# One decoder layer with 32 experts on one Trainium2 core: the first round of the expert stage in another order

## The reference, cut to what matters

```python
g_logits = (x @ w_rg + b_rg);  _, g_idx = lax.top_k(g_logits, 1)
e_logits = (x @ w_re + b_re).reshape(N, 4, 8)
e_sel = take_along_axis(e_logits, g_idx[:, :, None], axis=1)[:, 0]
e_val, e_idx = lax.top_k(e_sel, 2)
e_w = softmax(e_val) * take_along_axis(softmax(g_logits), g_idx)
for e in range(32):
    h = jax.nn.silu(x @ w_eg[e]) * (x @ w_eu[e])
    out = out + combine[:, e:e + 1] * (h @ w_ed[e])
```

## Time and profile before

| | us |
|---|---|
| median of 3 runs | 718.13 (714.38 to 722.01) |
| profiled execution, its own time | 714.71 |
| its span, first to last instruction | 712.9 |
| first matmul of the expert rounds, in the span | 143.40 |
| first slot of the ring loaded anew, in the span | 149.48 |
| last weights of experts issued | 629.06 |

### The profile page before, as it was taken

The page is one execution under the profiler, slowest core; times in us unless marked ns, Lnnn a source line. Parts: engine busy times, 40 slices in busy tenths (PEclk is TensorE's granted clock), DMA queues, the critical chain, the costliest instruction groups (busy, mean ns, idle before and its releaser), DMA issues.

```text
span 712.9 us, 8954 instructions
## 1 busy us (share of the span) xinstructions
PE 659.5 (93%) x2874; PEld 454.9 (64%) x2874; DVE 549.0 (77%) x595; ACT 478.3 (67%) x439; POOL 92.9 (13%) x123
## 2 busy tenths in 40 slices
PE   9999998789999999989999999898989899998895
PEld 4566554367767686766767677675767576674342
DVE  2265125948999999999999999998989899994543
ACT  3200203649878888798887979897877888881253
POOL 4000001200021120202202021120202020210000
PEclk9999999989999999999999999999999999999998
DMA  9993304359999999999999999999999999874401
GB/s 304 391 300 118 119 29 156 139 228 407 419 409 427 421 414 425 404 416 409 416 412 419 416 409 404 414 399 404 410 373 408 412 390 397 349 280 174 145 15 59
DMA packets 30750, 232.36 MB, mean 326 GB/s; under 512 B 8694, under 2 KB 10046, under 8 KB 17925
## 3 DMA queue, kind: packets, MB, share of 16 engines
q1 hardware_dynamic: 25277, 226.09, 79.4%
q0 software_dynamic: 4480, 5.26, 2.2%
q10 hardware_dynamic: 976, 0.79, 0.3%
HBM read 231.76 MB, written 10.37 MB: 340 GB/s over the span
## 4 chain that ended last, share of the span: by engine, by line
PE 50%; DMA 25%; DVE 10%; issue 9%; ACT 4%; DVEq 0%; POOLq 0%; SPq 0%; ACTq 0%; POOL 0%
DMA moe_rows<-yo,cur 18%; PE ps L841 9%; PE ps L842 8%; DMA ring<-in_w_eg_dram 6%; PE ps L915 5%; PE ps L752 5%; PE ps L856 5%; DVE lo L1429 5%; PE ps L844 4%; ACT hi L1024 3%; PE ps L653 2%; PE ps L660 2%; PE ps L647 2%; DVE yo L1422 2%; PE ps L614 2%
## 5 line engine op out<-in xcount | busy, mean ns | idle before, releaser
L1024 ACT ACTIVATE hi<-ring 128x2048 fp32r<-128x2048 f32 x192 | 318.4, 1698 | 24.1 <-PE ps L842 6.7
L1429 DVE TENSOR_TENSOR lo<-ring,hi 128x2048 fp32r<-128x2048 f32 (+1 forms) x128 | 256.2, 2022 | 27.4 <-ACT hi L1024 13.2
L841 PE MATMUL ps<-hi,xr 128*128 128x512 f32 x448 | 194.8, 435 | 17.1 <-DVE lo L1429 14.4
L1429 DVE TENSOR_TENSOR lo_third<-ring,hi 128x1536 fp32r<-128x1536 f32 (+1 forms) x64 | 129.3, 2020 | 6.5 <-ACT hi L1024 5.9
L842 PE MATMUL ps<-lo,xr 128*128 128x512 f32 x320 | 127.1, 397 | 0.0
L841 PEld LDWEIGHTS ps<-hi,xr 128*128 128x128 f32 x448 | 85.4, 191 | 47.6 <-DVE lo L1429 21.1
L841 PE MATMUL ps<-hi,hr 128*128 128x512 f32 x224 | 91.0, 406 | 12.3 <-DVE lo L1429 9.6
L1033 ACT ACTIVATE gu<-ps 128x512 f32<-128x512 f32 x64 | 70.0, 1094 | 23.3 <-PE ps L844 23.3
L856 PEld LDWEIGHTS ps<-fold,gu 128*128 128x128 f32 x512 | 61.9, 192 | 21.8 <-issue 13.7
L559 POOL DMA_INDIRECT moe_rows<-yo,cur x16 | 35.2, 2199 | 300.3 <-DVE yo L1422 300.3
L842 PEld LDWEIGHTS ps<-lo,xr 128*128 128x128 f32 x320 | 61.4, 192 | 12.0
(11 more groups left out here) (234 smaller groups left out, 625.5 us busy)
## 6 DMA issues: line engine op xcount, KB each, us to landing
ring<-in_w_eu_dram SPq DMA_DIRECT2D x32, 2048.0 KB, 18.2
ring<-in_w_eg_dram SPq DMA_DIRECT2D x32, 2048.0 KB, 17.6
ring<-in_w_ed_dram SPq DMA_DIRECT2D x31, 2048.0 KB, 18.8
ring<-in_w_in_dram SPq DMA_DIRECT2D x2, 2048.0 KB, 17.2
ring<-in_w_out_dram SPq DMA_DIRECT2D x2, 2048.0 KB, 21.4
ring<-in_w_ple_gate_dram SPq DMA_DIRECT2D x2, 2048.0 KB, 10.2
ring<-in_w_in_dram SPq DMA_DIRECT2D x2, 1024.0 KB, 8.8
ring<-in_w_ed_dram SPq DMA_DIRECT2D x2, 1024.0 KB, 7.9
```

Source lines behind the costliest of these rows:

```text
L841: mm(out, parts, hi(u)[:, cut], start=begin, stop=False)
L1024: acti(hi(u), ring[:, u // 2, off:off + split(u)], ACT.Copy).then_inc(hi_ready, counted(u, first, last))
L1429: V.tensor_tensor(lo(u), ring[:, u // 2, off:off + split(u)], hi(u).bitcast(F32), ALU.subtract).then_inc(lo_ready, counted(u, first, last))
```

## The change

All edits are at the seam between routing and the rounds.

1. DVE writes the first pair's row numbers straight into `cur` (not `row_in`), and POOL issues the first gather without its own copy. The wait of `all_slots` on POOL's copy goes.
2. POOL zeroes the pads after it has issued the first gather, not before.
3. PE does `ple_product(2)` ahead of the places, `(3)` and `(4)` after the first pick, then turns the gathered rows, and only then does the 48 products for the other pairs and `ple_product(5)`.
4. ACT copies product 4 and then `xr` ahead of unit 3's high part and product 5. It waits for `rows_r` before the first copy of a gate product.
5. DVE does `low_x(0)` after unit 0's low part, ahead of unit 1's and of `all_slots`.
6. In the first step ACT copies the up product (`copy_gu` of unit 3) ahead of unit 7's high part.

```diff
-                pool.wait_ge(hn_out, 16 * TILES)
-                pool.wait_ge(cur_in, x + 1)
+                pool.wait_ge(cur_in, q * PAIRS + i)
                 pool.sem_inc(turns, 1)
+                gather_rows()
+
+            def gather_rows():
+
                 nc.gpsimd.indirect_dma_start(
                     xg[0:ODD_END, :], None, hn_rows,
...
                 slot_numbers()
+                pool.wait_ge(hn_out, 16 * TILES)
+                need(pool, x_done, q * ROUNDS)
+                pool.wait_ge(rows_r, 2 * q + 1)
+                pool.sem_inc(turns, 1)
+                gather_rows()
                 if isinstance(q, int):
-                    pool.wait_ge(hn_out, 16 * TILES)
                     zero(xr[:, :, :, :, SLOTS:HALF].bitcast(F32), xz[:, :, SLOTS:P],
                          h32[:, :, SLOTS:P], hr[:, :, :, SLOTS:HALF].bitcast(F32))
-                pool.wait_ge(rows_r, 2 * q + 1)
-                pool.sem_inc(turns, 1)
-                gather(q * ROUNDS, 0)
...
-            ple_product(0)
-            ple_product(1)
+            for n in range(3):
+                ple_product(n)
...
                 pick_slots(q, 0)
                 if isinstance(q, int):
-                    ple_product(2)
                     ple_product(3)
+                    ple_product(4)
+                    pe.wait_ge(most_r, 1)
+                turn_x(q * ROUNDS)
                 pick_slots(q, 1)
                 if isinstance(q, int):
-                    ple_product(4)
                     ple_product(5)
-                pe.wait_ge(most_r, 1)
-                turn_x(q * ROUNDS)
                 pe.wait_ge(pads, 1)
...
-                    for u in range(2):
-                        high(u)
-                        copy_ple(2 * u)
-                        copy_ple(2 * u + 1)
-                    high(2, 3)
+                    high(0)
+                    copy_ple(0)
+                    copy_ple(1)
+                    high(1)
+                    copy_ple(2)
+                    copy_ple(3)
+                    high(2)
                     copy_ple(4)
-                    copy_ple(5)
                     act.wait_ge(pads, 1)
                     high_x(n)
+                    high(3)
+                    copy_ple(5)
+                    act.wait_ge(rows_r, 2)
...
-                    high(6, 7)
+                    high(6)
+                    if not first:
+                        high(7)
                     copy_gu(n, x, 3)
+                    if first:
+                        high(7)
...
-                V.tensor_tensor(row_in[:, 0:1], r_a[:, 0:1], ps[:, FIRST_IDX, 1:2], ALU.add).then_inc(rows_r, 1)
+                V.tensor_tensor(cur[:, 0:1], r_a[:, 0:1], ps[:, FIRST_IDX, 1:2], ALU.add).then_inc(rows_r, 1)
...
-                dve.wait_ge(cur_in, q * ROUNDS + 1)
...
                     choose(1, PAIRS)
-                    low(0, 1)
+                    low(0)
+                    low_x(0)
+                    low(1)
                     all_slots(0, link)
                     dve.wait_ge(ple_s, 2 * TILES)
                     low(2)
-                    low_x(0)
```

More of the change, by code:

```diff
@@ L536, in slot_numbers, with gather @@
                 nc.gpsimd.memset(slot_no[:, SLOTS:HALF], -NOWHERE).then_inc(iota_s, 1)
-            def gather(x, i):
+            def gather(x, i, q):
                 need(pool, x_done, x)
@@ L567, in step @@
                 if not last:
-                    gather(n + 1, i + 1)
+                    gather(n + 1, i + 1, q)
                 if not first:
```

## The result

| | before | changed |
|---|---|---|
| median of 20 runs | 719.32 us (713.42 to 723.42) | 716.24 us (714.0 to 718.89) |
| ratio | | 0.9958, 95% interval 0.9941 to 0.9976 |
| profiled execution, own time (span) | 714.71 (712.9) | 716.06 (714.3) |

The change is 3.0 us faster (1.7 to 4.2), where I had forecast 5.2: a gain clear of noise, of 0.4% and not 0.7%. Timed again beside other kernels it gave 0.9934 (0.9904 to 0.9963). The profiled execution of the changed kernel is an ordinary one; that of before is one of its kernel's fastest (714.71 against a median of 719.32), and so it is the shorter of the two. Two things have to be taken apart in the trace.

A forecast was written before the change was run, and what follows sets the result against it. DMA engines, unbroken from SP's first refill (149.48 us), bound the kernel. Unit 0 3.65 us sooner plus 1.55 by the clock gives 5.2 off the 718.13 us median: 712.9 us, range 706 to 720.5.

The forecast's parts named there:

- The mechanism: Rounds: DMA engines work without a pause from the first refill, so the end comes sooner by as much, 5.2 us.
- Rival A: Rounds: compute engines are the bound to the end, so 6.7 us gained, 711.4 us, up to 8; chance 0.17.
- Rival B: First gather: DVE's compare holds off POOL, rows come at 137.6, only 3.3 us gained, 714.8 us; chance 0.13.
- the signs that I had named: Trace after: for example, forecast wrong if first refill moves by 5 us and last weights' issue (629.06) does not.
- Rival C: Rounds: longer queue lowers DMA rate from 416 to 403 GB/s, 7.1 us lost against 5.2 gained, 720.0; chance 0.10.
- PE: Routing: product 2, 1.8 us, fits ahead of the places; turn at 135.7, picks until 137.9, product 5 until 139.7.
- The gather 0.99 after the row numbers: First gather: without POOL's copy its DMA begins 0.99 us after DVE's write, at 131.2, so 0.8 us earlier.
- Turn, picks and product 5: PE before unit 0: turn 135.7 to 136.65, picks until 137.9, product 5 (1.79 us) until 139.7.
- Units 0 and 1: First units on PE: 4.32 us instead of 5.89 with no hole ahead, 1.55 us gained by the clock.
- Pads: POOL's 18 memsets behind the first gather, 1.7 us in all: cost 0 to 0.3 us, at worst 2.
- The second gather's copy: POOL's copy beside unit 2's low part may be held until 143.9; nothing lost, as PE wants the rows about 160.
- about 1%: Measurement: 7.2 us is what can be told from no change; chances 0.26 faster, 0.67 within 1%, 0.07 slower.

The follow-up runs named there:

- e5: Changed kernel with the first refill held back until unit 3 is done, engines' work unchanged; 718.76 us, 0.9993 of before.
- the light transfers: Refills of rounds 1 to 15 cut to three quarters of their bytes (results wrong): changed kernel 693.07 us, kernel before 704.31 us.
- e1: Changed kernel with product 2 behind the first pick again; 713.3 us, 0.9924 of before.
- e2: Kernel before with only POOL's part: row numbers straight to `cur`, first gather ahead of the pads, turn still last; 718.26 us, 0.9991 of before.
- e7b: Kernel before with slot 2's down matrix for round 1 loaded already at 77 us; 719.75 us, 1.0004 of before.
- e6: `e1` with unit 7's high part again ahead of the copy of unit 3's up product; 715.46 us, 0.9939 of before.
- e7: `e1` with slot 2's down matrix for round 1 loaded already at 77 us; 710.15 us, 0.9880 of before.
- p3: The changed kernel itself, three products ahead of the places, timed again in another job; 715.03 us, 0.9934 of before.
- w1: Changed kernel with two extra unit-matrix products on PE around turning the last tile of h, ahead of the routing; 715.69 us, 0.9936 of before.
- p4: Changed kernel with product 3 also ahead of the places, four in all; 719.79 us, 0.9986 of before.

## Why the prediction was wrong, and where it was right

**The mechanism held in the main.** The time goes with the first refill as long as no pause follows, and the engines' further lead turns into queue: landing times at 200 us rose from 13.2 to 18.0, and `e5` and the light transfers show it. Rival A (engines to the end, 6.7 or more) is refuted by them, and by ACT's waits, which grew (6.4 us to 8.9 for the up matrices). Rival B, GpSimd held off by VectorE's comparison, did not occur: the gather's instruction took 1.15 us, and rows moved at 74 to 205 GB/s from 136.5 us on, with the comparison running until 138.3. Of the signs that I had named, one came out against me: the first refill moved, and the last weights' issue did not (629.08 against 629.06). In the other traces it did (625.22 in `e1`, 633.18 in `e2`).

Rival C came in small. From 180 to 400 us the rate is 416 GB/s in both kernels, but split up, the changed kernel has 421 from 180 to 320 us and 408 from 320 to 440, where before has 417 and 413. Over 180 to 620 us that makes 409 against 410, so the changed kernel lost next to nothing by it. The lower rate goes with the queue: from 320 to 440 us it was 412 or 413 in the traces whose up matrices landed in 16 to 17 us at 300 to 330 us (before, `e2`, `e7b`, `e6`, `e7`), and 403 to 410 where that took 19 to 21. My argument that 13 and 22 us differ only in how many transfers wait left this out.

**The step that failed** is the first one under **PE**: product 2 ahead of the places, "so it fits", costed at nothing beyond its 1.8 us at the full clock. By length it did fit: three products at the full clock put the places 5.26 us after the first product (`p3`, `w1`), and I had counted on 5.59. But in the trace after, the clock stood at 0.50 from 125 to 128 us, the products took 7.11 us, and the places came at 6.95, 1.36 late. I had written of the clock for the units and not for this place. Row numbers and gather were late by as much, the turn by 1.1, since the gather took 4.1 us and not 4.5, unit 0 by 1.0 and the first refill by 0.9:

| us after the first product | forecast | trace after |
|---|---|---|
| places | 5.59 | 6.95 |
| gather begins | 8.85 | 10.18 |
| turn | 13.35 | 14.44 |
| unit 0 | 17.40 | 18.37 |
| first refill | 21.95 | 22.89 |

There was also something to be had that I did not see: with two products ahead the places stand at 4.9, because the cast of VectorE that took 0.84 us beside the memsets now took 0.17. The room is 1.2 us ([1.21 <-DVE] with two products ahead), not 1.9, for a product of 1.8. With product 2 back the gain is 5.5 us (3.4 to 7.6) in one job and 7.7 (5.7 to 9.7) in the other, around and above my 5.2.

The Trainium skill (SBUF — State Buffer, section Who interferes with whom) says that a cast of VectorE can run in a mode in which it and GpSimd's instructions exclude each other. The trace agrees: 0.84 us beside the memsets, 0.17 without. I had looked at that section for what it would cost behind the gather, and not for what it gave back ahead of it.

**Other terms.** The gather 0.99 after the row numbers: as assumed. Turn, picks and product 5: 0.96, 1.18 and 1.86 against 0.92, 1.19 and 1.79. PE stood still for 1.95 us before the turn, not "up to a microsecond". Units 0 and 1: from 142.88 to the end of the last matmul at 147.21, 4.33 against 4.32, at the full clock, in this trace; in `w1` and `p4` part of them ran at the halved clock. Pads: free. The second gather's copy took 1.98 us and ended at 146.86, with VectorE's subtraction at 146.81: foreseen, and free. My "about 1%" for what can be told from no change was too coarse: 20 runs of each tell 0.42% to within 0.18%.

**What stays open.** Whether the full DMA engines hold the kernel up through the weights, as I argued, or also through the scatter, on which ScalarE waits longer, is not parted by any run. Of the 2.2 us between forecast and medians, the trace places 0.9 at the first refill. The rest is within the interval (1.7 to 4.2 us), and no run here shows where it went: behind the first refill the traces differ by more than that, 479.6 against 481.7 us to the last issue, and 83.8 against 85.2 from there to the end, which the change doesn't touch. The clock's level changes from one execution to the next at places that no kernel here controls, so one trace each can't settle the last microsecond.

## What to carry to other kernels

When a long stretch is full of transfers, cost a change first by the instant at which the stretch begins and by the pauses inside it. To test that the transfers set the end, hold one back that no engine needs yet: moving the engines and the transfers together can't tell. A transfer moved ahead of the stretch helps only as far as its room doesn't turn into a pause. Room for extra work in an engine's gap is the gap after the change: ask what ended it, and whether the same change makes that earlier. Work put into a gap ahead of a short dependent step should be costed at both levels of the clock: products 0 and 1 took 3.70 us in some traces and 5.40 in others, in the same place of the list.

## What the hardware showed that I had not expected

Runs of one kernel differ through the granted clock. The 35 runs of before in the first job had mean granted clocks of 0.971 to 0.985, and a line fitted to their spans falls by 0.56 us for each 0.001 of clock (correlation -0.88). The lower level came at different places in different executions: from 60 to 70 us the mean was 0.67 in the changed kernel's trace and 1.00 in that of before, with the same mixer.

A gather of up to 112 rows took 4.1 us from its instruction's start to landing when the DMA engines were idle, and 12.3 to 13.1 us in the rounds of these two kernels (the scatter of the results 11.3 to 11.7), whether the weights' queue was 13 or 22 us long.
